# Splitting freed weights four slots later in the attention of a hybrid encoder, and the low part of an input tile ahead of the weights'

## What is computed

```python
def c_mixer(x, norm_g, w_in, qn_g, kn_g, w_out):
    h = rms_norm(x, norm_g)
    q, k, v = jnp.split(h @ w_in, ...)            # 8 query, 2 key, 2 value heads of 128
    q = apply_axial_rope(rms_norm(q, qn_g), ...)
    k = apply_axial_rope(rms_norm(k, kn_g), ...)
    sc = jnp.einsum('bqkgd,bskd->bkgqs', qblk, k) * scale
    pr = jax.nn.softmax(sc, axis=-1)
    o = jnp.einsum('bkgqs,bskd->bqkgd', pr, v)
    return x + o @ w_out
```

## Time and profile before

| | us |
|---|---|
| median of three runs | 1729.49 |
| the profiled execution | 1732.63 |
| its span | 1730.9 |
| PE busy | 1660.8 |
| DVE busy | 1108.7 |
| ACT busy | 694.2 |
| POOL busy | 140.6 |
| entry of layer 1 and its attention, about | 878 to 1144 |

### The profile page before, as it was taken

One profiled execution on the slowest core, in us unless ns is written; L12 is line 12 of the kernel. 1 busy time (PEld: TensorE's weight loads), 2 busy tenths in 40 slices (PEclk: granted clock), 3 DMA queues, 4 the chain that ended last, 5 costly groups with the idle time before them and its releaser, 6 DMA issues.

```text
span 1730.9 us, 23952 instructions
## 1 busy us (share of the span) xinstructions
PE 1660.8 (96%) x9564; PEld 1596.4 (92%) x9564; DVE 1108.7 (64%) x1604; ACT 694.2 (40%) x1087; POOL 140.6 (8%) x79
## 2 busy tenths in 40 slices
PE   5999899999999999999999999889999999999997
PEld 5999888989999999999999777679999999999997
DVE  6432564687777577577643666668767757756764
ACT  4332333454244144144432555555434423423430
POOL 4000200210000000000223222212000000000000
PEclk8999989999999999999999999999999999999999
DMA  4122002222222222212211000012222232222222
GB/s 130 51 61 68 30 1 74 62 61 57 67 73 80 68 74 71 76 49 68 79 56 49 25 21 19 8 52 61 61 74 61 68 92 61 68 71 58 74 74 74
DMA packets 193902, 104.92 MB, mean 61 GB/s; under 512 B 3808, under 2 KB 191200, under 8 KB 193792
## 3 DMA queue, kind: packets, MB, share of 16 engines
q1 hardware_dynamic: 193312, 102.25, 20.7%
q0 software_dynamic: 144, 0.79, 0.1%
q10 hardware_dynamic: 336, 0.35, 0.1%
HBM read 100.23 MB, written 3.15 MB: 60 GB/s over the span
## 4 chain that ended last, share of the span: by engine, by line
PE 85%; DVE 6%; ACT 5%; issue 3%; DMA 0%; POOL 0%; ACTq 0%; DVEq 0%; SPq 0%; POOLq 0%
PE unit_ps L510 13%; PE unit_ps L512 12%; PE unit_ps L511 12%; PE unit_ps L784 12%; PE unit_ps L785 12%; PE unit_ps L786 12%; PE unit_ps L913 3%; PE misc_ps L510 1%; PE misc_ps L512 1%; PE misc_ps L511 1%; PE misc_ps L651 1%; ACT w_hi L1004 1%; DVE t L1603 1%; DVE h_pair L1577 1%; PE misc_ps L637 1%
## 5 line engine op out<-in xcount | busy, mean ns | idle before, releaser
L784 PE MATMUL unit_ps<-h_pair,w_hi 128*128 128x384 f32 x1232 | 413.7, 336 | 6.6 <-ACT t L1223 5.1
L785 PE MATMUL unit_ps<-h_pair,w_hi 128*128 128x384 f32 x1232 | 413.0, 335 | 0.0
L786 PE MATMUL unit_ps<-h_pair,w_lo 128*128 128x384 f32 x1232 | 412.8, 335 | 0.0
L510 PE MATMUL unit_ps<-pair_b,w_hi 128*128 128x384 f32 x960 | 324.8, 338 | 8.2 <-DVE pair_b L1669 4.1
L511 PE MATMUL unit_ps<-pair_b,w_hi 128*128 128x384 f32 x960 | 322.2, 336 | 0.0
L512 PE MATMUL unit_ps<-pair_b,w_lo 128*128 128x384 f32 x960 | 322.1, 335 | 0.0
L784 PEld LDWEIGHTS unit_ps<-h_pair,w_hi 128*128 128x128 f32 x1232 | 232.2, 188 | 7.8 <-ACT t L1223 5.8
L786 PEld LDWEIGHTS unit_ps<-h_pair,w_lo 128*128 128x128 f32 x1232 | 232.4, 189 | 0.0
L785 PEld LDWEIGHTS unit_ps<-h_pair,w_hi 128*128 128x128 f32 x1232 | 232.4, 189 | 0.0
L1004 ACT ACTIVATE w_hi<-w_raw 128x1024 fp32r<-128x1024 f32 x86 | 91.0, 1058 | 256.1 <-PE unit_ps L512 196.9
L510 PEld LDWEIGHTS unit_ps<-pair_b,w_hi 128*128 128x128 f32 x960 | 181.1, 189 | 11.9 <-DVE pair_b L1669 6.3
(11 more groups left out here) (230 smaller groups left out, 2300.7 us busy)
## 6 DMA issues: line engine op xcount, KB each, us to landing
w_raw<-in_w_gate SPq DMA_DIRECT2D x22, 512.0 KB, 3.9
w_raw<-in_w_up SPq DMA_DIRECT2D x22, 512.0 KB, 5.2
w_raw_more<-in_w_gate SPq DMA_DIRECT2D x22, 512.0 KB, 3.9
w_raw_more<-in_w_up SPq DMA_DIRECT2D x22, 512.0 KB, 5.2
w_raw<-in_w_down SPq DMA_DIRECT2D x24, 384.0 KB, 3.6
w_raw_more<-in_w_down SPq DMA_DIRECT2D x24, 384.0 KB, 3.6
w_raw<-in_ab_w_in SPq DMA_DIRECT2D x17, 512.0 KB, 4.0
w_raw<-in_c_w_in SPq DMA_DIRECT2D x12, 512.0 KB, 3.9
```

Of the source, the lines that this page charges most:

```text
L510: pe.matmul(out, w_hi, m_hi, start=start, stop=False)
L784: pe.matmul(out, hi, m_hi, start=starts and k == 0, stop=False, skip_group_check=True)
L785: pe.matmul(out, hi, m_lo, start=False, stop=False, skip_group_check=True)
L786: last = pe.matmul(out, lo, m_hi, start=False, stop=k == HK - 1, skip_group_check=True)
```

## The change

The splits that the end of a query unit allows, on ACT and on DVE, move from slot 0 of the next unit to its slot 4, behind everything else in that slot. The splits freed by the other seven units stay at slot 0. In the last `down` of layer 0, for the last input tile only, DVE makes the low part of the tile before the low part of the weights, and not after it.

```diff
+PREP_SLOT = {n: 4 for n, kind, _ in QK if kind == "q"}
...
-                if slot % 8 == 0 and 0 <= j < len(C_UNITS):
+                if slot - PREP_SLOT.get(slot // 8 - 1, 0) in range(8, 8 * len(C_UNITS) + 1, 8):
                     ahead(BASE["c"] + j)
...
-                    ahead(n)
+                    last = r is not None and f == KT - 1
+                    if not last:
+                        ahead(n)
                     if r is not None:
                         dve.wait_ge(unit_read, reads(n))
                         gain_lo(KT * (r // 2) + f, gain, pair, f)
+                    if last:
+                        ahead(n)
...
-                if slot % 8 == 0 and 0 < j <= len(C_UNITS):
+                if slot - PREP_SLOT.get(slot // 8 - 1, 0) in range(8, 8 * len(C_UNITS) + 1, 8):
                     ahead(BASE["c"] + j - 1)
```

## The result

The changed kernel took 1732.32 us, the median of 20 runs (1730.14 to 1736.82); the kernel before, run beside it, 1730.11 us (1719.93 to 1732.22). Paired on the same chips the ratio is 1.0026, with a 95% interval of 1.0013 to 1.0038: slower by some 4.5 us (2.2 to 6.6), which is within the 0.3% that the prediction took as its bound for "same". The forecast was 1735.7 us, 3.4 us too slow, and the time lies within its range.

What follows compares the result with a forecast made beforehand. PE, busy 96% of the span, bounds the kernel, with an ACT-DVE softmax chain behind its attention waits. Chain +7.74 us less 1.52 for the clock gives +6.2: 1735.7 us against the 1729.49 median; range 1727.5 to 1740.

Steps and rivals of the forecast that it cites:

- the chain's sum: Second layer's attention: heads 1 to 5 pay 1.22 us each, head 6 2.10, head 0 -0.46; together +7.74 us.
- the first rival: Attention: chain grows, but most value products run at 2.4 GHz; four falls lost 1731.2 us, all lost 1726.6; chance 0.30.
- the prediction's own signs of being wrong: Attention: heads under 23.9 us, granted clock 1.00 over several heads' value products, or `w_lo` of 2 us.
- the signs for the chain: Attention: DVE idle some 1.4 us before a 1.22 us `w_lo`, reciprocal behind; `probs_t` waits nearly gone in heads 1 to 5.
- Removal: Attention: without the split at slot 0, ACT reaches `probs_t` 0.95 us sooner, covering PE's 0.88 us wait.
- Insertion: Attention, slot 4: DVE's split waits for `w_hi` and delays the reciprocal of step 1, lengthening the softmax chain 2.10 us.
- What reaches PE: Attention: of the chain's 2.10 us, 0.88 is absorbed, so the value product moves 1.22 us per head.
- Entry: Second layer's entry: low part of last input tile before the weights' split; between -0.06 and 0, taken as 0.
- The clock: Value products of the attention: seven clock falls cost 1.52 us each; most stay, one taken as lost, -1.5 us.
- the two patterns: Before value products where the clock fell: sums and 0.88 us of waiting (second), or 1.95 us of waiting without sums (seventh).
- DVE is not held: Attention: `w_lo` ends before the exponential hands over, insertion costs nothing; 1724.2 us, or 1713.6 with all falls lost; chance 0.08.
- Slack in the chain: Attention: unseen slack lets only a rest of the 2.10 us arrive, gain and loss cancel; 1729.5 us, chance 0.05.

Runs made afterwards that it cites:

- the run at slot 2: Kernel before, with both ACT's and DVE's halves of the query units' splits moved to slot 2, under the value product: 1717.6 us, ratio 0.9921.
- the attention's part alone: Kernel before, with only the query units' splits moved to slot 4 on ACT and DVE, the entry unchanged: 1730.95 us, ratio 1.0011.
- the two experiments with a fill: Overwritten products before each long value product of the kernel before: 1720.28 us; before heads 6 and 7 only, with query and output units' splits at slot 2: 1713.2 us.

## Why the prediction was right in its chain, and which term was off

The direction was right and the chain's sum was right; the time was 3.4 us lower than forecast, chiefly because more of the clock's falls went than the sum took. That the time lies in the range says little by itself, since the range took in most of the first rival. And two of the prediction's own signs of being wrong came: heads under 23.9 us (23.45, twice, where about 25.0 was named) and a granted clock of 1.00 over the value products of three heads. They concern the clock's term; the signs for the chain came as forecast.

*Removal.* Right. The 0.88 us in front of six value products are gone, and two waits stay, as said.

*Insertion.* Right to 0.07 us, and nearer still since this head began 0.08 us later than in the trace before (1005.16 against 1005.08). Forecast were `w_lo` at 1007.06, 1.22 us long, and the reciprocal at 1008.20; the trace has 1007.13, 1.22 and 1008.27. The split took its price without a POOL instruction beside it, so the dearer row was rightly kept for the range alone. Two experiments show the cause: with `w_hi` ready the delay is 0.57 us, and one slot later on DVE the head is 1.63 us shorter.

*What reaches PE.* Right. The forecast was 1.22 us for a head with both parts; the lengths at full clock give 23.45 - 22.33 = 1.12. Head 0 was to gain 0.46: from the first product of the attention to the first value product it took 879.74 to 970.10, 90.36 us, where it took 90.87 before, a gain of 0.51. (The split alone did not hold the first maximum: it ended at 952.52, and two instructions on `q_scale` stood behind it. They moved up with it, so the sum is the same.) Head 6 was to pay 2.10. In the kernel before its window is

```profile
1090.55:1113.71 23.16, 19.82 (x87) 14.20 (x88) 15.50 (x34) 12.67 (x26) 6.26 (x4) 0.93 0.03 9
```

It is 24.60 us now, 1.44 more, while the clock gave back 0.07 x 23.16 - 0.04 x 24.60 = 0.64: 2.08 without the clock. Head 7, 20.97 us, is as before.

*Entry.* Right in its sum, nothing. Its working was off in one duration: the split there was taken at 1.22 us and took 2.86, beside a POOL instruction that began at 881.59. It ended at 884.61, which is 885.3 in the time of the trace before (0.68 us later here), and not near 883.7. The trace before already had that POOL instruction, from 882.28 to 884.23, and the prediction did not look for it. No wait of PE names the split, so the cover that the prediction named held.

*The clock.* This is the term that was mis-sized: "I take one lost: -1.5". The seven value products that fell took 36.8 us before (six at 5.16 to 5.26 and one at 5.40) and 30.8 after. Seven stretches at the lower level have become four: three are gone whole, two lie inside a value product as before (at 970.10 and 1115.58), and two begin in the weight products ahead of one (at 996.06 and 1090.98), which is why these took 4.31 and 4.63. The windows just ahead of these two:

```profile
995.00:996.00 1.00, 1.00 (x4) 1.00 (x4) 0.00 (x0) 0.98 (x3) 1.00 (x1) 0.50 0.00 0
1090.00:1091.00 1.00, 1.00 (x5) 1.00 (x5) 0.00 (x0) 0.98 (x3) 0.99 (x1) 0.50 0.00 0
```

Since the clock is also low in parts of a head outside that product, the windows are the safer sum: (1 - granted clock) x length is 11.65 us before (0.07 x 142.41 for six heads and 0.08 x 20.97) and 6.70 after, so about 4.95 us came back (an estimate, as the clock is printed with two digits), some 3.3 falls of 1.52 us where one was taken. The step that failed is the inference "it does not hang on one pattern, so these rows say that most stay": the two patterns had a wait before the value product in common, and in the run at slot 2, where the wait went and the sums stayed, six of six value products behind it kept the higher clock. With the 4.95 the working closes: the chain's 5 x 1.22 + 2.10 = 8.20 from the first to the last value product, less 4.95, is 3.25, against 3.07 measured.

The runs say the same without a trace. At a mean granted clock of 0.981 the kernel before took 1729.7 to 1730.7 us (12 runs beside two experiments) and the changed one 1736.0 to 1736.8 (4 runs); at 0.984 to 0.985, 1722.5 to 1722.8 (5 runs) and 1730.1 to 1732.4 (11 runs). At a like clock the change costs 6 to 9 us, about the 7.74 of the sum. The kernel before ran mostly at 0.980 to 0.981, the changed one mostly at 0.983 to 0.985, and so the medians lie closer. The profiled execution of the changed kernel is one of its four at 0.981; at the median more of the clock's time was regained than the trace shows.

The Trainium skill, "TensorE: Matmul & The Clock Gate", section "What's actually happening", has the throttled clock as the default that activity releases. The prediction weighed it against the rows and leaned on the rows. The experiment that filled the wait agrees with the page: products in a gap that PE would have idled through gave 0.9944. But the falls did not all go when the gap went, neither in the changed kernel (four value products of eight were slow, three of them without a wait in front) nor in the one with the fill, so the page's direction held, and the sum that the prediction drew from it with all falls lost, -2.9, did not.

*The rivals.* "The clock stays up" asked for four falls lost and 1731.2 us; with 3.3 falls back and 1732.3 us the result lies nearer to it than to the forecast. The two share the chain and differ in the clock alone. "DVE is not held" is excluded: DVE stood 1.42 us idle before the split. Where its condition was nearly built, with ACT's half two slots ahead and the reciprocal only 0.57 us late, the kernel was faster than before (0.995), so its mechanism was sound and its condition was what failed. "Slack in the chain" is excluded by the 1.12 of 1.22 us that reached the value product.

*Open.* Which heads lose their fall was not settled. It changes from execution to execution: in the attention's part alone six of eight value products ran at 3.70 us, in the changed kernel, with the same attention, four; and the seventh, behind the same 1.95 us of waiting, took 3.70 us in the one and 5.40 in the other. And the two experiments with a fill each kept a fall at a value product that began without a wait, so the wait in front of it is not a fall's only cause.

## What to carry to other kernels

In a chain that two engines pass back and forth, an instruction put between one engine's hand-over and the other's costs its own length plus the wait for its input, less the slack that stood there; here 1.22 us of work cost 2.10, of which some 1.5 was that wait. Before a background operation is moved, look for a point where both engines are idle under a long piece of PE's work, and check that the operand from the other engine is ready there: the same split cost 1.12 us a head at slot 4 and gained 0.95 at slot 2. If its place can't be changed, moving the consumer's half one step later than the producer's takes out most of the price.

## What was not expected of the hardware

A wait of 0.88 us on PE cost more by the clock than by itself: filling it, with no other change, gave 0.9944, some 10 us over the run, though PE spent each wait's time on the added products: about the 10.6 us of seven falls at 1.52 us each. In the profiled execution the stretch of the attention was 7.9 us shorter, with one head of 24.58 us that kept a fall.

The same kernel runs at different mean clocks. The kernel before ranged from 0.978 (1735.5 to 1735.9 us) to 0.987 (1720.2 us), with the changed kernel's 1.0026 lying well inside that spread: a difference of a few tenths of a per cent here needs runs at a like clock, or the trace.

The split of 128x1024 took 1.22 us alone, 2.00 beside POOL, and 2.86 at the entry. The timelines of POOL, after the change at the entry, and before it about the second head's value product:

```profile
881.59 1.93 POOL L1831 TENSOR_TENSOR sumsq<-sumsq,t 128x768 f32<-128x768 f32 x1 [4.29 <-ACT t L1028]
...
993.66 1.82 POOL L1867 TENSOR_TENSOR pair_b<-t,pair_b 128x768 fp32r<-128x768 f32 x1 [4.96 <-ACT pair_b L1294]
995.62 2.60 POOL L1862 TENSOR_TENSOR t<-t,ropes 128x768 f32<-128x768 f32 x1
```

At the entry POOL's instruction lasted from 881.59 to 883.52, and the split ended 1.09 us after it, nearly its whole length alone. Before, the split at 994.57 met an instruction that ended at 995.48, and it ended 1.09 us later too, at 996.57. The next one of POOL began in that time and took 2.60 us, where the same line takes 1.80 in the changed kernel (at 996.74), with no split beside it. So each delayed the other, and in the attention the change took this meeting away, which is where POOL's 5.7 us and most of DVE's 6.5 went. The Trainium skill, "SBUF — State Buffer", section "Who interferes with whom", says that the port pair that DVE and GpSimd (POOL here) share is an exclusive lock, so that the second to come is blocked and not slowed; the 1.09 us behind POOL's end, twice, agree with it.
